# A Mamba-2 mixer plus mixture-of-experts layer: the state's share of the mixer output moved from a scaled C to a plain C with a decay factor applied afterwards

## What is computed

```
y_diag = einsum('btsg,btsgj,bsgj,bsgjp->btgjp', cb, decay, dtk, xk)
y_off  = einsum('btgn,bgjpn,btgj->btgjp', ck, state, jnp.exp(acum))
y      = y_diag + y_off + d_skip * x,  then  y * silu(z),  RMS norm per group, w_out
```

## Time and profile before

| | us |
|---|---|
| median of 3 runs (1170.88 to 1173.53) | 1172.5 |
| the profiled execution's own time | 1168.81 |
| its span in the profile | 1166.7 |
| PE busy | 1027.9 (88%) |
| DVE busy | 940.1 (81%) |
| ACT busy | 628.2 (54%) |
| POOL busy | 493.8 (42%) |

### The profile page before, as it was taken

How to read it: one execution, slowest core, us unless ns; L and a number is a source line. 1 busy time by engine, 2 the same in 40 slices (tenths; PEclk the granted TensorE clock), 3 DMA queues, 4 the chain that set the end, 5 groups by cost and what they waited for, 6 DMA issues and landing times.

```text
span 1166.7 us, 15729 instructions
## 1 busy us (share of the span) xinstructions
PE 1027.9 (88%) x5234; PEld 842.1 (72%) x5234; DVE 940.1 (81%) x1005; ACT 628.2 (54%) x584; POOL 493.8 (42%) x308
## 2 busy tenths in 40 slices
PE   0798899999988997975899999999999999999960
PEld 0577679777977986845688887788777788878850
DVE  6687973995598377876788989888998898998868
ACT  1354452445236335244477677776776667777640
POOL 1343544544464344201726534355354654446210
PEclk9899989999999998977899999999999999999995
DMA  9232423432451334335789999999999999999963
GB/s 363 64 117 76 146 72 115 138 90 85 127 166 54 96 123 168 132 117 211 279 319 364 369 351 357 356 374 353 349 359 352 370 354 362 366 359 371 361 253 145
DMA packets 101755, 279.39 MB, mean 239 GB/s; under 512 B 9961, under 2 KB 57233, under 8 KB 84319
## 3 DMA queue, kind: packets, MB, share of 16 engines
q1 hardware_dynamic: 95850, 270.65, 64.0%
q0 software_dynamic: 4496, 8.19, 2.0%
q10 hardware_dynamic: 1382, 0.21, 0.1%
HBM read 274.51 MB, written 12.58 MB: 246 GB/s over the span
## 4 chain that ended last, share of the span: by engine, by line
DVE 20%; DMA 19%; PE 13%; issue 10%; ACT 6%; POOL 1%; DVEq 0%; SPq 0%; ACTq 0%; POOLq 0%
DVE moe_r L1172 10%; DMA moe<-in_moe_w_down 9%; DMA moe<-in_moe_w_up 9%; ACT moe_r L781 5%; DVE moe L1279 1%; PE ps L1713 1%; PE ps L1717 1%; PE ps L1715 1%; DVE moe_r L1285 1%; DVE moe_r L1273 1%; PE ps L1424 1%; PE ps L1426 1%; PE ps L1425 1%; PE ps L1665 1%; PE ps L1664 1%
## 5 line engine op out<-in xcount | busy, mean ns | idle before, releaser
L1172 DVE TENSOR_TENSOR moe_r<-moe,moe_r 128x2048 fp32r<-128x2048 f32 x192 | 444.0, 2332 | 67.5 <-ACT moe_r L781 66.2
L781 ACT ACTIVATE moe_r<-moe 128x2048 fp32r<-128x2048 f32 x192 | 368.1, 1921 | 178.0 <-DMA moe<-in_moe_w_up 101.8
L1713 PE MATMUL ps<-moe_r 128*128 128x512 f32 x768 | 224.8, 401 | 19.7 <-DVE both L968 12.0
L1715 PE MATMUL ps<-moe_r 128*128 128x512 f32 x768 | 218.9, 394 | 0.0
L1717 PE MATMUL ps<-moe_r 128*128 128x512 f32 x768 | 218.0, 393 | 0.0
L500 POOL TENSOR_TENSOR ssd_r<-ssd,ssd_r 128x1024 fp32r<-128x1024 f32 x56 | 138.2, 2469 | 142.1 <-ACT ssd_r L625 137.3
L1713 PEld LDWEIGHTS ps<-moe_r 128*128 128x128 f32 x768 | 140.3, 190 | 53.1 <-DVE both L968 12.0
L1717 PEld LDWEIGHTS ps<-moe_r 128*128 128x128 f32 x768 | 145.7, 190 | 31.6
L1715 PEld LDWEIGHTS ps<-moe_r 128*128 128x128 f32 x768 | 145.7, 190 | 31.5
L578 POOL DMA_INDIRECT ydram<-moe,moe_i x16 | 35.4, 2213 | 260.9 <-DVE moe L1291 236.2
L1424 PE MATMUL ps<-ssd_r 128*128 128x512 f32 x320 | 133.4, 417 | 11.6 <-DVE ssd L916 9.8
(11 more groups left out here) (284 smaller groups left out, 1520.0 us busy)
## 6 DMA issues: line engine op xcount, KB each, us to landing
moe<-in_moe_w_up SPq DMA_DIRECT2D x128, 1024.0 KB, 6.7
moe<-in_moe_w_down SPq DMA_DIRECT2D x64, 1024.0 KB, 8.2
ssd<-in_ssd_w_in SPq DMA_DIRECT2D x40, 512.0 KB, 3.9
ssd<-in_ada_w SPq DMA_DIRECT2D x30, 512.0 KB, 3.5
ssd<-in_ssd_w_out SPq DMA_DIRECT2D x16, 512.0 KB, 3.5
ssd<-in_ada_w SPq DMA_DIRECT2D x4, 1024.0 KB, 9.7
early<-in_ada_w SPq DMA_DIRECT2D x4, 1024.0 KB, 11.6
moe<-ydram SPq DMA_DIRECT2D x8, 512.0 KB, 5.2
```

Of the source, the lines that this page charges most:

```text
L781: act.activation(wr[:, i % RING, 0, :], ring[:, i % RING, :], ACT.Identity).then_inc(s_wh, 1)
L1172: dve.tensor_tensor(wr[:, i % RING, 1, :], ring[:, i % RING, :], wr[:, i % RING, 0, :].bitcast(F32), ALU.subtract).then_inc(s_wl, 1)
L1713: mm(to[i], xh, wh[i], start=start, stop=False)
L1715: mm(to[i], xh, wl[i], start=False, stop=False)
```

## The change

POOL's `decayed_c` is gone, and with it the semaphore `s_ch` on which ACT and PE waited. PE forms, for a pair of heads and a chunk, one product of the whole 128 columns of state with plain C, into bank 4 or 5 instead of the output bank. ACT's second exponential writes only the head's own 64 partitions, so that the two heads of a pair make one tile `grow[q]` whose rows match the product. DVE's `gate` multiplies product and `grow` (384 columns), and adds the result to its own first step. The SiLU that writes next C (tile 1) moves behind the last squares, since PE now reads C until `y_pair(3)`. In the last turn the three products of the modulation come before the transposes, and a transfer of a modulation piece waits for the new semaphore.

```diff
+        chflat = ch.rearrange("p h t -> p (h t)")
+        grow = [ebc[:, 0, :], ebc[:, 1, :], chflat[:, 0:T], chflat[:, T:2 * T]]
+        offtmp = chflat[:, 2 * T:2 * T + T - P]
...
                 elif k == 3:
-                    sp.wait_ge(s_y, 4 * G)
+                    sp.wait_ge(s_off, 4 * G + 1)
...
-            def decayed_c(g, h):
-                pool.wait_ge(s_e, HG * g + h + 2)
-                if h >= 4:
-                    pool.wait_ge(s_y, 4 * g + (h - 4) // 2 + 1)
-                pool.tensor_tensor(ch[:, h % 4, :], cT[:, P:], ebc[:, h % 2, P:], ALU.mult).then_inc(s_ch, 1)
...
-                if h >= 2:
-                    act.wait_ge(s_ch, HG * g + h - 1)
-                act.activation(ebc[:, h % 2, :], bank(2 + h % 2), ACT.Exp).then_inc(s_e, 1)
+                half = slice(h % 2 * HD, (h % 2 + 1) * HD)
+                act.activation(grow[h // 2][half, :], ps[half, 2 + h % 2, :], ACT.Exp).then_inc(s_e, 1)
...
                     turn_unit(g, 7)
-                    silu(g + 1, 1)
                 square(g, 2)
                 square(g, 3)
+                if not last:
+                    silu(g + 1, 1)
...
                 dve.scalar_tensor_tensor(yt, xT[:, q, :], gnd[:, 1, q:q + 1], bank(6 + q % 2), ALU.mult, ALU.add).then_inc(s_y1, 1)
+                dve.wait_ge(s_e, HG * g + 2 * q + 3)
+                if q:
+                    dve.wait_ge(s_ya, 4 * g + q)
+                dve.tensor_tensor(offtmp, ps[:, 4 + q % 2, P:], grow[q][:, P:], ALU.mult).then_inc(s_off, 1)
                 dve.wait_ge(s_y1, 4 * g + q + 1)
+                dve.wait_ge(s_off, 4 * g + q + 2)
+                dve.tensor_tensor(yt[:, P:], yt[:, P:], offtmp, ALU.add).then_inc(s_ya, 1)
+                dve.wait_ge(s_ya, 4 * g + q + 1)
                 dve.tensor_tensor(yT[:, q, :], yt, yT[:, q, :], ALU.mult).then_inc(s_yz, 1)
...
             def y_pair(g, q):
-                pe.wait_ge(s_ch, HG * g + 2 * q + 2)
...
                 if q >= 2:
                     pe.wait_ge(s_y1, 4 * g + q - 1)
+                    pe.wait_ge(s_off, 4 * g + q)
                 for k in range(TT):
+                    if k:
+                        mm(ps[:, 4 + q % 2, k * P:(k + 1) * P], state[:, k - 1, q * P:(q + 1) * P], cT[:, k * P:(k + 1) * P], start=True, stop=True)
                     for hh in range(2):
                         h = 2 * q + hh
-                        o = ps[hh * HD:(hh + 1) * HD, 6 + q % 2, k * P:(k + 1) * P]
-                        op = mm(o, xdt[:, k, h * HD:(h + 1) * HD], mh[:, h % 4, k, :], start=True, stop=(k == 0))
-                        if k:
-                            op = mm(o, state[:, k - 1, h * HD:(h + 1) * HD], ch[:, h % 4, (k - 1) * P:k * P], start=False, stop=True)
+                        op = mm(ps[hh * HD:(hh + 1) * HD, 6 + q % 2, k * P:(k + 1) * P], xdt[:, k, h * HD:(h + 1) * HD], mh[:, h % 4, k, :], start=True, stop=True)
...
             def last_projection():
+                pe.wait_ge(s_e, HG * G + 1)
+                for k in range(3):
+                    mod_piece(k)
                 pe.wait_ge(s_bcu, 2 * (G - 1) + 1)
+                pe.wait_ge(s_off, 4 * G + 1)
...
                 op.then_inc(s_modt, 1)
-                pe.wait_ge(s_e, HG * G + 1)
-                for k in range(3):
-                    mod_piece(k)
...
                 pe.wait_ge(s_stu, 3 * g + 1)
+                pe.wait_ge(s_off, 4 * g + 1)
```

More of the change, by code:

```diff
@@ L244, in build @@
         s_st, s_stu, s_stm = sems("s_st s_stu s_stm")
-        s_abc, s_seg, s_dec, s_e, s_m, s_ch = sems("s_abc s_seg s_dec s_e s_m s_ch")
+        s_abc, s_seg, s_dec, s_e, s_m, s_off, s_ya = sems("s_abc s_seg s_dec s_e s_m s_off s_ya")
         s_y, s_y1, s_yz, s_sq, s_sqs, s_ms = sems("s_y s_y1 s_yz s_sq s_sqs s_ms")
@@ L512, in _ @@
             pool.memset(oacc, 0.0)
-            def decayed_c(g, h):
-                pool.wait_ge(s_e, HG * g + h + 2)
-                if h >= 4:
-                    pool.wait_ge(s_y, 4 * g + (h - 4) // 2 + 1)
-                pool.tensor_tensor(ch[:, h % 4, :], cT[:, P:], ebc[:, h % 2, P:], ALU.mult).then_inc(s_ch, 1)
             def turn(g, last):
-                heads_after = {1: (0, 1), 2: (2,), 3: (3,), 4: (4, 5), 5: (6, 7)}
                 for i in range(TU - (XU if last else 0)):
                     unit_low(TU * g + (XU + i), i % 2, wlate[i - 6] if last and i >= 6 else None)
-                    for h in heads_after.get(i, ()):
-                        decayed_c(g, h)
                     if i == (5 if last else 7):
@@ L667, in exps @@
                 act.activation(seg[:, h % 2], seg[:, h % 2], ACT.Exp).then_inc(s_dec, 1)
-                if h >= 2:
-                    act.wait_ge(s_ch, HG * g + h - 1)
-                act.activation(ebc[:, h % 2, :], bank(2 + h % 2), ACT.Exp).then_inc(s_e, 1)
+                half = slice(h % 2 * HD, (h % 2 + 1) * HD)
+                act.activation(grow[h // 2][half, :], ps[half, 2 + h % 2, :], ACT.Exp).then_inc(s_e, 1)
             def square(g, q):
                 act.wait_ge(s_yz, 4 * g + q + 1)
-                if q == 0:
-                    act.wait_ge(s_ch, HG * g + HG)
                 act.activation(squares[q], yT[:, q, :], ACT.Square).then_inc(s_sq, 1)
@@ L868, in _ @@
         def _(dve):
-            for s in (s_oacc, s_var, s_stu, s_adau, s_yl, s_bcu, s_ye):
+            for s in (s_off, s_oacc, s_var, s_stu, s_adau, s_yl, s_bcu, s_ye):
                 dve.sem_inc(s, 1)
```

## The result

The changed kernel takes 1188.18 us (median of 4 runs, 1183.91 to 1189.04). The kernel before, on the same chip, takes 1172.34 (4 runs, 1170.88 to 1173.53). The ratio is 1.0128, with a 95% interval of 1.0101 to 1.0156: slower, by 15.8 us of the medians.

A forecast was written before the change was run, and what follows sets the result against it. PE was taken to bound the mixer, its wait before tile 4 set by DVE's gates. Three hardware turns +13.9, last turn +3.3, clock +1.5 make 18.7 on 1168.81: 1187.5 us, range 1168 to 1197.

The forecast's parts named there:

- the case forecast as the likeliest: The whole kernel slower, at 1176 to 1195 us; chance 0.60.
- The start of gate 0: DVE's heads, freed of stalls beside POOL's dropped product, let gate 0 start 1.4 us earlier a turn (bounds 0 and 2.9).
- The gate: DVE's new 384-column product and addition, 0.59 each, make every gate 1.07 us longer, 4.3 a turn.
- contention: DVE's gate operations stretched beside POOL's: 3.55 us a turn against 2.4 before, +1.2 (bounds -2.4 and +2.5).
- SiLU's +0.55: On ACT, SiLU of tile 1 now stands ahead of the high parts and adds 0.55 us a turn.
- The clock in the hardware turns: PE's wait before tile 4 grows from 2.7 to about 6 us; the lower clock behind it adds 0.5 a turn.
- The last turn: Gate 0's start gains 0; gate 3 ends at 463.2 instead of 459.95, +3.3 us; modulation products fit in before.
- The switches: PE's passages between half and full width, three there and back a pair: 0.24 us each, +0.7 a pair, mostly covered.
- the prediction's other reading: A full wait at each PE width switch: a pair loses 1.0 us, not 0.7, altering the last turn alone, by 0.5.
- Slower, and more: Rival, chance 0.15: lower clock lasts two stretches behind longer waits, switches drain in full; 8 to 12 us more, 1196 to 1200.
- Faster: Rival, chance 0.16: all 8.0 us of stretching in DVE's heads go, gate 0 starts 8.0 earlier; total 1164 to 1168.
- No difference: Rival, chance 0.09: gate 0 starts 4 to 6 us earlier, or gates lie in slack; total within 2 us of before.

The follow-up runs named there:

- e3: The kernel before without POOL's product (plain C, decay left out) and with SiLU of tile 1 behind the last square: 1156.97 us, ratio 0.9858.
- e4: The kernel before with two meaningless 384-column operations added to each gate on DVE, POOL's product kept: 1189.18 us, ratio 1.0146.
- e5: e1 with SiLU of tile 1 moved between the last two squares: 1181.51 us, ratio 1.0084 to the kernel before.
- e2: The changed kernel without the gates' two new DVE operations, so the state's share never reaches the output: 1167.46 us, ratio 0.9955 to the kernel before.
- e1: The changed kernel with each pair's three full-width products grouped ahead of its eight half-width ones: 1180.99 us, ratio 1.0061 to the kernel before.
- e6: e5 with the first steps of gate 0 ahead of the wait for SiLU of z: 1176.13 us, ratio 1.0052 to the kernel before.
- e8: The kernel before with only gate 0's first step moved ahead of the wait for SiLU(z): 1157.42 us, ratio 0.9901.

## Why the prediction was right, and where it was not

The total was forecast at 1187.5 and came out at 1188.18, inside its range, and the case forecast as the likeliest came true. But the closeness is luck. Of the 18.7 us that were forecast for the mixer, 12.4 came: the three hardware turns were forecast at +15.4 with the clock and came to +5.3, the last turn at +3.3 and came to +7.1. The other 8.2 between the spans lie outside the mixer, where nothing was forecast, and only 1.6 of them are traced to the change. And the sum stood on an execution of before that lies 3.5 us below the median.

**The start of gate 0: the first step that failed.** It was forecast 1.4 us earlier in the turn and came 3.5 earlier, outside the bounds of 0 and 2.9. The mechanism was right, the size was not. In the second turn, operation by operation against before, these changed by over 0.3 us: a state step (L952 before) from 1.21 to 0.69, two L935 from 1.50 to 0.68 and 0.69, a piece (L943) from 3.36 to 1.28, and a copy (L905 before) from 0.97 to 0.16; one more L943 became 0.67 longer, from 1.28 to 1.95. DVE's last rows of the heads in the changed kernel, against the earlier trace rows:

```profile
243.82 1.28 DVE L934 SCALAR_TENSOR_TENSOR ssd<-ssd,both 128x1024 f32<-128x1024 f32 x1
245.02 0.69 DVE L926 TENSOR_TENSOR ssd<-ssd 128x512 f32<-128x512 f32 x1
...
247.09 1.95 DVE L934 SCALAR_TENSOR_TENSOR ssd<-ssd,both 128x1024 f32<-128x1024 f32 x1
```

The piece that took 3.36 takes 1.28, as the forecast had it. But the forecast then let POOL stop the next L935 until L500 was done. It was the other way round: the L926 of 245.02 takes 0.69, and the L503 of 244.20 takes 3.77. POOL paid, and DVE lost only the 0.67 of the next piece. With the state step and the copy, which the working of the 1.4 had left out, the sum over the heads is -4.0, of which 0.5 turn into rest: 0.24 behind a `mix_head`, and 0.27 at gate 0, whose wait for SiLU of z is 1.17 where it was 0.90. e3 shows it by itself: 4.05 earlier. Of the 10.1 us by which the hardware turns stayed under their forecast of 15.4, this step took 5.1: gate 0 came 2.3, 3.5 and 3.5 earlier in the three turns, so 0.9, 2.1 and 2.1 beyond the forecast. The chain took 1.1 (below), and what follows gate 3 the other 3.9: forecast +1.05 a turn for SiLU and clock, it came to -0.8, +0.4 and -0.2.

**The gate.** +1.07 for each gate and +1.2 for contention make 5.5 a turn; measured were 5.11, and 5.07 in e4. The price of 0.59 for the product and for the addition was 0.55 and 0.56. Contention came where it was put: 2.78 at gate 0, 0.69 at gate 2 and 1.38 at gate 3, forecast as 3.0, 0.94 and 1.5; in sum it grew by 0.6 and not 1.2. The Trainium skill's rule ("SBUF — State Buffer", on who interferes with whom) agrees: the addition, with two SBUF inputs, was stretched, and the product that reads PSUM never was (mean 550 ns).

**ACT.** SiLU's +0.55 was there (e5 takes 0.5 off tile 4's start) but was worth nothing where it was taken away: what that gave, the clock took. That compensation was not foreseen, nor that PE would wait for POOL's product and not for the taps.

**The clock in the hardware turns.** +0.5 a turn was forecast. In the second turn it is 35.64 us from tile 4's start to the turn's end, before 35.6: nothing. Over the three turns the lower clock took 18.5 us, before 20.4, so it cost about 1 us less and not 1.5 more. The wait grew to 3.7 and not to 5 to 7; the 2.1 by which gate 0 came earlier than forecast account for most of that.

**The last turn: the second step that failed.** Forecast +3.3, measured +7.1. The forecast let gate 3 and the low parts set the start of `last_tiles`, with PE's products of the modulation fitting in before. It was PE: from the third pair on it has no gap, and the low parts were done at 479.0, 1.5 before `last_tiles`.

```profile
475.76 3.24 DVE L1052 SCALAR_TENSOR_TENSOR ssd_r<-ssd,ssd_r 128x512 fp32r<-128x512 f32 x4 [1.31 <-ACT ssd_r L705]
480.49 0.48 PE L1522 MATMUL ps<-ssd_r 128*128 128x512 f32 x1
```

In PE's order: the third pair starts 1.4 later in the turn (0.9 of it because gate 0 does, which was forecast at 0), the two pairs take 4.1 longer (9.2 less 5.1), and what stands between them and `last_tiles` 1.6 longer. The DVE part alone was forecast at 2.3 and is 2.8 in e4; in the changed kernel it hides behind PE (e2: 0.4). The switches were under-priced, 0.24 where about 0.33 to 0.35 was measured, and so the pair: 2.65 us in the loop where 2.2 to 2.4 was forecast. With the prediction's other reading, a full wait each way, a pair would have lost 0.9 to 1.0; it lost 1.0 (2.65 less 1.63). The Trainium skill ("TensorEngine Tiling (Array Packing)", key properties) says that a change of mode drains the engine, without a figure. The trace agrees that each change of width costs time (0.78 us for a chunk whose records take 0.45). The clock was the larger omission: the forecast gave the third pair's switches +1.0 at the lower clock and the fourth's nothing, and the lower clock lasted through both and into the products of the modulation. e1 and e2 together show that this is the products' order, not the gates.

**The rest.** 1.6 us just behind the last turn belong to a low stretch (481.4 to 484.8) over `last_tiles`. The other 3.4 in the experts and the 3.3 before the first turn are not shown to come from the change: over the ten kernels the rest is 701.5 to 710.0 us, without order (e5, whose mixer differs little from e1's, has the highest, e1 the lowest), and the mixer starts at 97.5 to 98.6 in all but the changed kernel and e5 (101.0 and 101.2). So 14.0 of the 20.6 us between the two spans are traced to the change (5.3 + 7.1 + 1.6); the medians differ by 15.8. What moves the prelude and the experts stays open: with one profiled execution of each kernel it can't be said whether it goes with the kernel or with the execution. The clock doesn't explain it: within the rest it stood at the lower level for 72.0 us before (701.8), 74.4 in the changed kernel (706.8) and 70.0 in e5 (710.0).

**The rivals.** *Slower, and more* had its mechanism in the last turn (a longer low stretch and dearer switches) but not in the loop. *Faster* asked for a start 6.05 earlier; it was 3.5. e3 shows how near it lay: without the gate's operations the relief is worth some 4 to 6 us a turn. *No difference* asked for 4 to 6 earlier, and e6 came near it (4.7 against before; turns 0.1, 0.3 and 1.8 shorter, the last one 1.5 longer): its mixer takes as long as before within 0.6 us, while its total stays slower by 0.5%, by the rest.

## What to carry to other kernels

An operation dropped from an engine that nobody waits for can still be worth microseconds, through the operations of another engine that it stalls: count all of those from the groups (busy time against the undisturbed duration), not the few near the path. Replacing it by work on the engine that is the path cost more than that (18.0 against 12.7 us in the hardware turns, e2). Before moving work between engines, look for a wait that stands ahead of steps that don't need it: moving one such wait, and with it one operation by a fraction of a microsecond out of the way of a POOL product, brought 12.5 us here, more than half of it perhaps through the clock. And don't alternate between half-width and full-width products on PE; group them.

## What the runs showed of the hardware that was not expected

- PE lost about 0.33 us for each switch from half to full width and back (0.78 for a chunk where the records take 0.45), or 1.0 us in a pair; grouped, the two kinds of a pair took 1.8 (e1, second turn).
- With the alternating products PE counts as busy for 15.95 of 16.00 us and was nonetheless granted 0.62 of the clock in the mean, in the changed kernel and in e2 alike; the low stretch, which began in the wait ahead, lasted 13.7 us, and with the same products grouped, or the old ones, 6.8.
- Beside a POOL product a copy of 5 columns with a single SBUF input was stretched too, from 0.16 to 0.97 (L905 before).
- An earlier start can be given back to the clock (e5), and a wait shortened from 2.7 to 0.2 can bring 4.0, as the low stretch goes with it (e8).
